# The two middle blocks' gate projections in seven products, half of their 31-tap convolution summed in PSUM, and a new order behind them

## What is computed

```
proj = h @ w_in            # q, k, v, iq, ik, iw, a_in, c_in, g_in
q, k = partial_rope(rms_norm(q)), partial_rope(rms_norm(k))
rel = relu(iq . ik);  score = sum over heads of rel * iw       # index scores
idx = top_k(score, 64);  y_attn = attention(q, k, v over idx) @ w_attn_out
a = causal_dwconv(a_val * sigmoid(a_gate), 31 taps) + bias
y_conf = silu(layer_norm(a)) @ w_conf_out
y_sc = (c_b * causal_dwconv(c_c * c_x, 3 taps)) @ w_sc_out
gates = sigmoid(g_in)      # three gates of width 1024
x = x + (gates[0] * y_conf + gates[1] * y_attn + gates[2] * y_sc) @ w_o
x = x + (silu(u_gate) * u_val) @ w_down    # u = dwconv(norm(x) @ w_up)
```

## Time and profile before

| | us |
|---|---|
| median of 3 runs | 2019.89 (2019.89 to 2020.93) |
| profiled execution, its own time | 2019.41 |
| its span, first to last instruction | 2017.6 |
| mean granted TensorE clock in it | 1.000 (2.4 GHz) |

### The profile page before, as it was taken

The page is one execution under the profiler, slowest core; times in us unless marked ns, Lnnn a source line. Parts: engine busy times, 40 slices in busy tenths (PEclk is TensorE's granted clock), DMA queues, the critical chain, the costliest instruction groups (busy, mean ns, idle before and its releaser), DMA issues. The chain is left out here.

```text
span 2017.6 us, 34732 instructions
## 1 busy us (share of the span) xinstructions
PE 2003.7 (99%) x13230; PEld 1836.6 (91%) x13230; DVE 1055.7 (52%) x2702; ACT 403.7 (20%) x986; POOL 782.2 (39%) x537
## 2 busy tenths in 40 slices
PE   9999999999999999999999999999999999999999
PEld 7788889888889999999888888999999999899998
DVE  4244446974343567514992454557823366555541
ACT  2231521112111222111122122032202014220000
POOL 1000042000002487765000000668875774248873
PEclk9999999999999999999999999999999999999999
DMA  5314444344334455444444433444454443345444
GB/s 209 128 45 144 146 149 148 132 152 146 132 140 142 151 170 169 172 146 161 134 147 150 146 128 123 170 165 168 162 173 148 145 147 105 126 146 183 171 159 136
DMA packets 42960, 298.32 MB, mean 148 GB/s; under 512 B 4928, under 2 KB 6080, under 8 KB 8832
## 3 DMA queue, kind: packets, MB, share of 16 engines
q1 hardware_dynamic: 42560, 295.42, 42.7%
q10 hardware_dynamic: 256, 0.92, 0.3%
HBM read 294.35 MB, written 1.05 MB: 146 GB/s over the span
## 5 line engine op out<-in xcount | busy, mean ns | idle before, releaser
L708 PE MATMUL bank<-xn,ring 128*128 128x256 f32 (+2 forms) x3776 | 686.4, 340 | 0.5 <-DMA ring<-wstream 0.5
L708 PEld LDWEIGHTS bank<-xn,ring 128*128 128x128 f32 x3776 | 610.2, 190 | 69.0 <-issue 4.6
L708 PE MATMUL bank<-arena,ring 128*128 128x128 f32 (+2 forms) x3702 | 641.4, 328 | 4.3 <-DVE arena L1711 2.4
L708 PEld LDWEIGHTS bank<-arena,ring 128*128 128x128 f32 x3702 | 564.2, 191 | 62.3 <-issue 3.5
L708 PE MATMUL bank<-arena 128*128 128x128 f32 (+3 forms) x2264 | 298.1, 287 | 0.0
L708 PEld LDWEIGHTS bank<-arena 128*128 128x128 f32 (+1 forms) x2264 | 274.9, 192 | 9.3 <-issue 1.5
L708 PE MATMUL bank<-arena,h_res 128*128 128x128 f32 x1960 | 234.5, 276 | 1.9 <-POOL h_res L1676 1.2
L708 PEld LDWEIGHTS bank<-arena,h_res 128*128 128x128 f32 x1960 | 225.7, 192 | 4.5 <-POOL h_res L1676 2.4
L1711 DVE SCALAR_TENSOR_TENSOR arena<-arena,par (+2 forms) x536 | 214.6, 475 | 0.3
L1667 POOL TENSOR_TENSOR h_res<-ring 128x512 f32<-128x512 f32 x12 | 15.5, 1294 | 495.2 <-issue 363.0
L1672 POOL TENSOR_TENSOR arena<-ring 128x1024 f32<-128x1024 f32 (+1 forms) x70 | 167.0, 2385 | 89.7 <-DMA ring<-wstream 89.7
(11 more groups left out here) (224 smaller groups left out, 1624.6 us busy)
## 6 DMA issues: line engine op xcount, KB each, us to landing
ring<-wstream SPq DMA_DIRECT2D x264, 1024.0 KB, 4.8
ring<-wstream SPq DMA_DIRECT2D x16, 768.0 KB, 4.2
cst<-consts SPq DMA_DIRECT2D x1, 2488.0 KB, 14.7
h_res<-tokens SPq DMA_DIRECT2D x2, 544.0 KB, 5.3
out<-arena SPq DMA_DIRECT2D x4, 256.0 KB, 5.4
arena<-arena ACTq DMA_DIRECT2D x4, 160.0 KB, 3.8
ring<-wstream SPq DMA_DIRECT2D x2, 288.0 KB, 2.8
par<-params SPq DMA_DIRECT2D x1, 541.5 KB, 9.2
```

Of the source, the lines that this page charges most:

```text
L708: return pe.matmul(o, lhs, rhs, start=start, stop=stop, skip_group_check=True)
```

## The change

- The stage `g` (12 blocks, one per 256 gate columns) replaces `g0`, `g1a` and `g1b` and is in seven-product form: `mix` on POOL, `first_product` on ACT, `unite` on DVE, then tanh on ACT over the united pair in SBUF. It runs in one piece.
- The convolution's loop has two passes, for tiles 0 to 3. Tiles 4 to 7 are taken in pairs by `convolved(lo, hi)`: the running sum lies in bank 4 (`both_p`), and only the last tap writes to SBUF. It makes 124 taps (4 tiles x 31): 28 before the gates and 8 behind each of the 12 `unite`s, the last 8 behind the last.
- `take("beside", ...)` rotates over banks 5 to 7. It is used from `row_sums` to `row_spread` and for the variance.
- TensorE's order behind the gates: `row_spread`, `cx0`, `centre_sums`, index scores, `cx1`, variance, `cb`. ACT, DVE and POOL follow in theirs: the squares stand between ACT's evictions of `cx0` and the relus; `x_res` is scaled behind the index rotation; the mean is subtracted ahead of the scores; the q/k rotation, top-k, the three-tap convolution (out of the heads) and the layer norm come behind the scores, in this order.
- `cb` is multiplied on DVE straight from its banks (`branch_b`), with no eviction by ACT.
- Eight products on zeros at the start where there were six (16 instructions for 12).

```diff
@@ -106,9 +106,7 @@
         pl(n + "ik", "w_in_2", l, 1, 1, 8, lambda it, q: span(iko, 72))
-        pl(n + "g0", "w_in_2", l, 3, 2, 8, seq(go))
-        pl(n + "g1a", "w_in_2", l, 1, 2, 8, seq(go + 1536))
-        pl(n + "g1b", "w_in_2", l, 2, 2, 8, seq(go + 2048))
+        fast(n + "g", "w_in_2", l, 12, 1, lambda it, q: go + 256 * it)
         pl(n + "cx0", "w_in_2", l, 2, 2, 8, two(co + 1024, co + 2048))
         pl(n + "cx1", "w_in_2", l, 2, 2, 8, two(co + 1536, co + 2560))
         pl(n + "cb", "w_in_2", l, 2, 2, 8, seq(co))
...
+FAST = [f"L{l}.{part}" for l in range(2) for part in ("a", "g", "attn", "o", "up", "down")] 
@@ -396,6 +394,9 @@
 
     def take(self, kind, key):
 
+        if kind == "beside":
+            self.turn["side"] += self.turn["side"] % 4 == 0
+            kind = "side"
         b = self.turn[kind] % 4 + (4 if kind == "side" else 0)
         self.turn[kind] += 1
         what = f"use{b}"
...
@@ -1066,33 +1067,24 @@
-                row_sums(L + "qk", 10, "pick", 1)
+                row_sums(L + "qk", 10, "pick", 1, "beside")
...
-                blocks(L + "g0", 8, x256, S)
-                blocks(L + "g1a", 8, x256, S)
-                row_spread(L + "qk", 5, 1)
+                fast_stage(F, "g", 12, 1, of_tokens(xn), (F, "x"), None)
+                row_spread(L + "qk", 5, 1, "beside")
+                blocks(L + "cx0", 8, x256, S)
                 centre_sums(L + "ln", 1, lambda j: sel[:, 0, :], [(L + "ln", "total")])
-                blocks(L + "g1b", 8, x256, S)
...
-                blocks(L + "cx0", 8, x256, S)
-                blocks(L + "cx1", 8, x256, S)
 
                 pe.wait_ge(*e.at((L + "ikr",)))
...
@@ -1107,7 +1099,15 @@
                             ins = mm(b, slice(0, P), slice(S * s_, S * s_ + n),
                                      iq0[rows, 2 * j2 + s_, P * t:P * t + P], ik[rows, 0, 0:n])
                         ins.then_inc(*e.side_done((L + "idx", t, j)))
-                blocks(L + "cb", 8, x256, S)
+                blocks(L + "cx1", 8, x256, S)
+                b = e.take("beside", (L + "ln", "var"))
...
+                for q in range(4):
+                    halves(L + "cb", q, 8, [P, P], x256, S)
                 for event in [(L + "yc", j) for j in range(ND)]:
                     pe.wait_ge(*e.at(event))
...
@@ -1447,23 +1433,33 @@
-                gates(L + "g0", 0)
-                gates(L + "g1a", 12, 1)
+
+                def gate_tanh_l(it):
+
+                    for part in ("c11", "c12", "c22"):
+                        act.wait_ge(*e.at(((F, "g", it, 0), part)))
+                    act.activation(flat(sg[:, 2 * it:2 * it + 2, :]), flat(sg[:, 2 * it:2 * it + 2, :]), ACT.Tanh,
+                                   scale=0.5).then_inc(*e.step((F, "sg", it)))
+
+                for it in range(12):
+                    first_product((F, "g", it, 0))
+                    if it >= 1:
+                        gate_tanh_l(it - 1)
+                gate_tanh_l(11)
                 for p in range(5):
                     act.wait_ge(*e.at((L + "qkn", p)))
                 for a, b in ((0, 16), (16, 0)):
...
-                centred_squares(L + "ln", 8, lambda j: ac[:, j, :])
-                gates(L + "g1b", 16, 2)
-                root((L + "ln", "var"), sq[:, 0, 0:S], D, RMS_EPS, (L + "ln", "rms"))
-                for j in range(8):
-                    act.wait_ge(*e.at((L + "z", j)))
-                    act.activation(ac[:, j, :], yc[:, j, :], ACT.Tanh).then_inc(*e.step((L + "zt", j)))
-                for c in range(2):
+
+                def products_in(c):
...
                     with e.turns(f"{L}cx{c}", 2) as i:
...
+
+                products_in(0)
+                centred_squares(L + "ln", 8, lambda j: ac[:, j, :])
                 for t in range(2):
...
@@ -1474,12 +1470,11 @@
                         two = psum[b][:, :].rearrange("p (r n) -> p r n", r=2)[:, :, 0:n]
                         dst = rel[:, j % 2, :].rearrange("p (r n) -> p r n", r=2)[:, :, 0:n]
                         act.activation(dst, two, ACT.Relu).then_inc(*e.frees((L + "idx", t, j), (L + "rel", t, j)))
-                act.wait_ge(*e.at((L + "yc", ND - 1)))
-                with e.turns(L + "cb", 2) as i:
...
-
+                products_in(1)
+                root((L + "ln", "var"), sq[:, 0, 0:S], D, RMS_EPS, (L + "ln", "rms"))
+                for j in range(8):
+                    act.wait_ge(*e.at((L + "z", j)))
+                    act.activation(ac[:, j, :], yc[:, j, :], ACT.Tanh).then_inc(*e.step((L + "zt", j)))
@@ -1685,19 +1680,19 @@
-                    if L == "L0" and b == ("L0", "attn", 0, 0):
+                    if L == "L0" and b == ("L0", "g", 0, 0):
                         pool.memset(iq[:, :, :], 0.0).then_inc(*e.step(("iq", "zero")))
-                    if b == (L, "attn", 0, 0):
-                        for n in range(4):
-                            pool.wait_ge(*e.at_turn((L + ".ac",), n))
...
-                        gather(L + ".ln", S, sq)
                     if b[0] == L:
                         mix(b)
+                    if b[0] == L and b[1] == "g":
+                        for j in {3: (1,), 6: (2, 3), 11: (4, 5, 6, 7)}.get(b[2], ()):
+                            one = ac[:, 0, :] if j == 1 else sel[:, 0, :]
+                            event = (L + ".ln", "total") if j == 7 else (L + ".ln", "part", j)
+                            pool.wait_ge(*(e.at_turn((L + ".ac",), j // 2) if j < 4 else e.at((L + ".ac", j))))
+                            pool.tensor_tensor(out=sel[:, 0, :], in0=one, in1=ac[:, j, :], op=ALU.add).then_inc(*e.step(event))
+                            pool.wait_ge(*e.at(event))
+                    if b == (L, "g", 11, 0):
+                        gather(L + ".ln", S, sq)
@@ -2184,7 +2179,7 @@
                 dve.wait_ge(*e.at((F, "cp", 2)))
 
                 dve.memset(tmp[:, 0, 0:S], 0.0).then_inc(*e.step((L + "qk", "zero")))
-                with e.turns(L + "conv", 4) as i:
+                with e.turns(L + "conv", 2) as i:
...
@@ -2195,10 +2190,23 @@
                             dve.wait_ge(*e.last(1))
                             stt(tile(ac, j), tile(cp, j)[:, k:k + S], G(g("conf_conv_w_2"), CK * j + k), tile(ac, j),
                                    ALU.mult, ALU.add).then_inc(*e.step((L + "ac",)))
-                if l == 0:
-                    invert("N3")
-                    for j in range(ND):
-                        dve.tensor_tensor(x_res[:, j, :], x_res[:, j, :], inverse("N3"), ALU.mult).then_inc(*e.step(("N3", "xn", j)))
+
+                def convolved(lo, hi):
+
+                    for n in range(lo, hi):
+                        j, k = 4 + 2 * (n // (2 * CK)) + n % 2, n % (2 * CK) // 2
+                        acc, weight = both_p[:, n % 2, :], G(g("conf_conv_w_2"), CK * j + k)
+                        if k == 0:
+                            if n >= 2 * CK:
+                                dve.wait_ge(*e.at((L + "ac", j - 2)))
+                            dve.tensor_scalar(acc, cp[:, j, 0:S], weight, G(g("conf_conv_b_2"), j), ALU.mult,
+                                              ALU.add).then_inc(*e.step((L + "tap", j, k)))
+                        else:
+                            dve.wait_ge(*e.at((L + "tap", j, k - 1)))
+                            stt(ac[:, j, :] if k == CK - 1 else acc, cp[:, j, k:k + S], weight, acc, ALU.mult,
+                                ALU.add).then_inc(*e.step((L + "ac", j) if k == CK - 1 else (L + "tap", j, k)))
+
+                convolved(0, 28)
                 rows_inverse(L + "qk")
                 dve.wait_ge(*e.at(("pe", (L + "ik",))))
                 b = e.bank_of((L + "ik",))
...
@@ -2210,28 +2218,19 @@
+                for it in range(12):
+                    unite((F, "g", it, 0), sg[:, 2 * it:2 * it + 2, :], 0)
+                    convolved(28 + 8 * it, 36 + 8 * it)
                 spread_norm(L + "qk", 5, lambda p: g("q_norm_g_2" if p < 4 else "k_norm_g_2"), qk0, qk0, L + "qkn")
-                centred(L + "ln", 8, lambda j: ac[:, j, :])
-                dve.wait_ge(*e.at((L + "ln", "rms")))
...
                 dve.wait_ge(iq_halves, 64 * (l + 1))
                 rotate_in_place(iq0[:, :, :], iq[:, :, :], "idx", slice(0, P), (L + "iqr",))
-                dve.wait_ge(qk_halves, 32 * (l + 1))
-                rotate_in_place(qk0[0:32, :, :], qk[0:32, :, :], "attn", slice(0, 32), (L + "rotated",))
...
-                for j in range(ND):
...
+                if l == 0:
+                    invert("N3")
+                    for j in range(ND):
+                        dve.tensor_tensor(x_res[:, j, :], x_res[:, j, :], inverse("N3"), ALU.mult).then_inc(*e.step(("N3", "xn", j)))
+                    for j in range(ND):
+                        dve.wait_ge(*e.at(("N3", "xn", j)))
+                centred(L + "ln", 8, lambda j: ac[:, j, :])
                 dve.wait_ge(*e.at((L + "iws",)))
...
+
+                dve.wait_ge(qk_halves, 32 * (l + 1))
```

(78 more changed lines are left out.)

53 lines of the change are left out of this document (7 added, 46 removed).

## The result

| | us |
|---|---|
| before, median of 5 | 2019.89 (2019.79 to 2020.93) |
| changed kernel, median of 5 | 2029.43 (2029.11 to 2032.58) |
| ratio | 1.0051, 95% interval 1.0037 to 1.0065 |
| predicted | 2017.6, range 2010 to 2024 |

The change costs 9.5 us, and the time lies 5 us above the range. The profiled execution took 2032.58 (span 2030.8, granted clock 0.991), 13.2 more than that of before; the other four ran at a clock of 0.992 to 0.993.

A forecast was written before the change was run, and what follows sets the result against it. TensorE, busy 99%, was taken to bound the kernel. Savings of 16.3 us against two waits per layer (3.2 and 3.7) and 0.2 of warm-up gave -2.3 us: median 2017.6, range 2010 to 2024, the forecast's own 2015.0 to 2020.4.

The forecast's parts named there:

- Term 1: Gates: seven-product blocks take 6.25 us for 6.91, and an old 0.51 us wait goes; together 16.3 us saved.
- Term 2: Row spreads: TensorE waits before the fourth until VectorE frees a bank, 3.2 us per layer, bounds 3.0 and 3.4.
- Term 3: Fifth index-score group waits for ScalarE's first relu; with a second wait behind it 3.7 us per layer, bounds 2.7 and 4.3.
- The second bound: Branch b's third block waits for a bank that VectorE empties late, 3.1 to 4.3 us; overlaps the index-score wait.
- The rest: Other moved work on VectorE costs nothing; the longer warm-up costs 0.2 us.
- Warm-up: Start of the kernel: 4 more instructions cost 0.2 us, bounds 0 and 0.5.
- the clock falls in the new gaps: Rival: slow stretches of 2.5 us behind four new gaps add 10 us, giving 2027.6; chance 13%.

The follow-up runs named there:

- e4: Changed kernel with spreads used before the last 8 taps, mean subtraction and squares behind scores and relus, branch b's first two products reordered on VectorE: 2002.49 us, ratio 0.9917.
- e3: Changed kernel with the mean's subtraction and its squares moved behind the index scores and relus: 2024.56 us, ratio 1.0021.
- e5: Kernel before with eight products on zeros at the start in place of six, nothing else: 2020.55 us, ratio 1.0.
- e1: Changed kernel with idle TensorE products filling the waits ahead of the fourth row spread and fifth index-score group: 2020.08 us, ratio 1.0001.
- e6: Changed kernel with about half of each new wait filled by idle TensorE products (3 and 4): 2026.28 us, ratio 1.0031.
- e9: e4 with one artificial wait per middle layer, five GpSimd additions, ahead of the fifth index-score group: 2020.14 us, ratio 0.9998.
- e10: e4 with one artificial wait per middle layer, five GpSimd additions, ahead of the second c-projection: 2014.44 us, ratio 0.9971.
- e2: Changed kernel with the use of the row spreads moved directly behind the last join, ahead of the last 8 taps: 2020.79 us, ratio 1.0004.
- e7: Kernel before with one wait per middle layer ahead of its two c-projections, made by four unused GpSimd additions: 2030.24 us, ratio 1.0046.
- e8: Kernel before with one wait per middle layer ahead of its two c-projections, made by three unused GpSimd additions: 2027.38 us, ratio 1.0036.

## Why the prediction was wrong, step by step

- **Term 1 right.** 6.26 us a block for the 6.25 predicted, no wait in the gates in either layer, and e4 gets the whole 16.3. VectorE held the pace: its eight PSUM taps take 3.23 us (0.404 each), and it then waits 1.2 us for TensorE, about the 1 us in hand. Timelines of the changed kernel, VectorE in the last gate blocks and GpSimd beside the first of these rows:

```profile
454.40 3.23 DVE L1706 SCALAR_TENSOR_TENSOR bank<-arena,par,bank 128x256 f32<-128x256 f32 x8 [0.20 <-DVE arena L2112]
...
460.65 3.23 DVE L1706 SCALAR_TENSOR_TENSOR bank<-arena,par,bank 128x256 f32<-128x256 f32 x8 [0.20 <-DVE arena L2112]
...
465.30 0.29 DVE L2106 TENSOR_TENSOR partial<-bank,p1c 128x128 f32<-128x128 f32 x1 [1.23 <-PE bank L709]
```

```profile
454.06 2.40 POOL L1667 TENSOR_TENSOR arena<-ring 128x1024 f32<-128x1024 f32 x1 [1.09 <-DMA ring<-wstream]
```

- **Term 2 right.** The place, the releaser and 3.15 us for 3.2.
- **Term 3 right in place and releaser, short in size.** 4.25 and 4.15 us for 3.7, within the outer 4.3 but above the 3.9 of this wait alone (3.7 by its own terms, 0.9 + 3.84 + 0.8 - 1.8; the sum gave 0.2 too much). The subtraction took longer than the row of L1 that I took as the long end, 4.36 us for 3.84, in both layers, beside GpSimd's additions. Timelines of VectorE and GpSimd:

```profile
504.39 4.36 DVE L2059 TENSOR_TENSOR arena<-arena,tmp 128x256 f32<-128x256 f32 x8
```

```profile
505.77 4.37 POOL L1635 TENSOR_TENSOR sq<-sq 128x256 f32<-128x256 f32 x5 [34.37 <-ACT sq L1237]
```

  The Trainium skill, SBUF — State Buffer, section SBUF: two separate sides, has a VectorE instruction with two SBUF inputs and a GpSimd one exclude each other. The trace agrees: eight subtractions cost 2.77 where GpSimd starts late and 4.36 here. In L1 of before the additions began 1.9 us behind the start of the subtractions, here 1.4 us behind it. No run takes the additions away. The second bound, at branch b, did not show in the changed kernel, since TensorE came later than I had it; e3 shows that it was real.
- **The rest nearly right.** Warm-up nil (e5), no other wait. Not in the sum: the index scores' 1.0 us less in their new place. It and the 1.0 us by which term 3 was too short cancel, by luck.
- **The step that failed: the sum takes each new wait at its length alone.** The slow clock behind it is put at nothing there and left to the rival "the clock falls in the new gaps", at 13%. The runs showed 13.7 us of slow clock behind the four gaps, and all 9.5 us of the loss gone when the gaps are filled (e1). The rival's 2027.6, with four stretches of 2.5 us, comes within 2 us of the 2029.43, partly by luck, since the stretches run from 1.7 to 5.1. I held against it one gap of 2.41 us that was followed by full rate. That was one execution of one gap, shorter than every new one, and even this gap drops the clock in some executions: it did in three of the twelve profiled ones (changed kernel, e5, e6), and before's own executions have mean clocks from 0.998 to 1.000. The warm-up row had shown the half rate after idling, so the rows at hand allowed the drop and excluded nothing. It should have been the forecast: 2017.6 + 10 = 2027.6.
- **The size of a stretch** was taken alike for all four. It is 1.7 to 2.9 at the spreads and 4.0 to 5.1 at the scores, where it depends on the work behind the gap (e9, e10). The median execution stands 9.5 us above before's and the profiled one 13.2. The stretch near 240 us can be 1.7 of that difference; the rest isn't split up, since only one execution has a trace.

## What to carry to other kernels

A wait on a TensorE that is otherwise full is priced at its length plus a stretch at 1.2 GHz behind it: here 1.5 to 5.1 us for each gap from 3.0 us on, so a wait of 3 us cost 5 to 6 and one of 4 between 6 and 9. A change that shortens TensorE's work and opens a few such waits can lose all of its gain, and the cure is order on the other engines: e4 moves a handful of VectorE and ScalarE steps and turns +9.5 us into -17.8. Where a gap can't be removed, idle products that fill it give back the clock part (e1), and here the place to leave one was ahead of the projection's 128-row products and not ahead of the 64-row ones of the scores (e10 against e9, 5.7 us apart).

## What the runs showed of the hardware

- The clock fell at every traced gap of 3.0 to 4.2 us, sixteen in all (changed kernel, e2, e3, e7, e9, e10). At gaps of 2.4 to 2.5 us it fell in some and not in others: at that near 240 us in three of twelve traces, and at one of two within one execution of e8. Gaps of 1.7 to 2.3 us passed in e6's trace, while the clocks of most of its other executions tell of drops.
- A gap that lost the clock cost 1.5 to 1.8 us of slow clock ahead of a projection (gaps of 2.5 to 4.1 us) and 4.0 to 5.1 ahead of the index scores (3.6 to 4.2 us).
- A sum kept in PSUM by VectorE, with one SBUF input, wasn't slowed by GpSimd's differences next to it: eight taps in a row take 3.23 us with them (454.40) and without (460.65). Subtractions with two SBUF inputs went from 0.35 to 0.55 us each beside GpSimd's additions.
- Thirty-two index-score products took 4.49 us in the new place without waits and 4.97 in the old one. Why wasn't looked into.
